# Feed-forward of a three-layer block: the first product takes both token halves together

## What is computed

```python
def sqrelu_mlp(h, w1, w2):
    return jnp.square(jax.nn.relu(h @ w1)) @ w2

    x = x + sqrelu_mlp(rms_norm(x, norm_ffn), w1, w2)   # w1: 1024 x 4096, w2: 4096 x 1024
return rms_norm(x, final_norm)
```

## Time and profile before

| | |
|---|---|
| time, median of 3 (lowest to highest) | 2796.82 us (2793.5 to 2798.48) |
| span of the profiled execution | 2797.9 us |
| TensorE busy | 2662.8 us, 95% |
| its weight loads | 2224.8 us, 80% |
| VectorE busy | 1160.3 us, 41% |
| ScalarE busy | 853.9 us, 31% |
| feed-forward's matmuls | from 2088.69 us to about 2790.3 us |

### The profile page before, as it was taken

One profiled execution on the slowest core, in us unless ns is written; L12 is line 12 of the kernel. 1 busy time (PEld: TensorE's weight loads), 2 busy tenths in 40 slices (PEclk: granted clock), 3 DMA queues, 4 the chain that ended last, 5 costly groups with the idle time before them and its releaser, 6 DMA issues. The chain is left out here.

```text
span 2797.9 us, 36557 instructions
## 1 busy us (share of the span) xinstructions
PE 2662.8 (95%) x13360; PEld 2224.8 (80%) x13360; DVE 1160.3 (41%) x2217; ACT 853.9 (31%) x1567; POOL 419.4 (15%) x890
## 2 busy tenths in 40 slices
PE   7999999998997999999979899999889999999998
PEld 6888888887786987777767588887668888888887
DVE  4433333323322410566644566665333333333333
ACT  4322222212212422444433443442332211122112
POOL 3444444432000204000001011011000000000000
PEclk9999999999998999999989899999899999999999
DMA  4211111102422221011034101100433111111111
GB/s 152 69 59 47 58 47 58 47 24 82 149 106 81 90 83 51 33 40 36 19 119 145 65 31 50 57 24 33 150 117 128 38 45 51 46 60 40 42 52 67
DMA packets 71391, 188.38 MB, mean 67 GB/s; under 512 B 7744, under 2 KB 29184, under 8 KB 70400
## 3 DMA queue, kind: packets, MB, share of 16 engines
q1 hardware_dynamic: 71296, 187.11, 20.3%
HBM read 149.34 MB, written 37.75 MB: 67 GB/s over the span
## 5 line engine op out<-in xcount | busy, mean ns | idle before, releaser
L527 PE MATMUL ra_qkv_ps<-ra_wh,ra_xl 128*128 (+1 forms) x512 | 206.7, 404 | 3.9 <-DVE ra_wl L420 3.9
L2513 PE MATMUL ff_f_ps<-x_upper,ff_w1l 128*128 128x512 f32 x512 | 200.5, 392 | 6.5 <-DVE ff_w1l L2449 6.5
L527 PE MATMUL ra_qkv_ps<-ra_wh,ra_xh 128*128 (+1 forms) x512 | 200.3, 391 | 0.0
L2513 PE MATMUL ff_f_ps<-x_lower,ff_w1h 128*128 128x512 f32 x512 | 200.2, 391 | 0.0
L2513 PE MATMUL ff_f_ps<-x_upper,ff_w1h 128*128 128x512 f32 x512 | 200.1, 391 | 0.0
L527 PE MATMUL ra_qkv_ps<-ra_wl,ra_xh 128*128 (+1 forms) x512 | 199.9, 390 | 0.0
L2526 PE MATMUL ff_y_ps<-ff_w2h,ff_hl 128*128 128x512 f32 x512 | 199.2, 389 | 0.0
L2526 PE MATMUL ff_y_ps<-ff_w2l,ff_hh 128*128 128x512 f32 x512 | 199.2, 389 | 0.0
L2526 PE MATMUL ff_y_ps<-ff_w2h,ff_hh 128*128 128x512 f32 x512 | 199.2, 389 | 0.0
L2476 DVE TENSOR_TENSOR ff_acc<-ff_y_ps,ff_acc 128x1024 f32<-128x1024 f32 x64 | 78.4, 1225 | 213.9 <-PE ff_y_ps L2526 213.9
L527 PE MATMUL ra_gate_ps<-ra_wh,ra_xl 128*128 (+1 forms) x512 | 156.0, 305 | 0.0
(11 more groups left out here) (391 smaller groups left out, 6582.2 us busy)
## 6 DMA issues: line engine op xcount, KB each, us to landing
staging<-in_w_ff SPq DMA_DIRECT2D x64, 512.0 KB, 3.9
ra_raw<-in_w_in_a SPq DMA_DIRECT2D x32, 768.0 KB, 4.6
gated_a<-ra_sg SPq DMA_DIRECT2D x64, 128.0 KB, 1.9
staging<-in_w_out_a SPq DMA_DIRECT2D x16, 512.0 KB, 3.8
staging<-in_w_vr_c SPq DMA_DIRECT2D x16, 512.0 KB, 4.0
wa_gin<-gated_a SPq DMA_DIRECT2D x6, 1024.0 KB, 5.0
staging<-in_x SPq DMA_DIRECT2D x8, 512.0 KB, 3.9
wa_xin<-in_x SPq DMA_DIRECT2D x8, 512.0 KB, 4.6
```

Source lines behind the costliest of these rows:

```text
L527: last = pe.matmul(out, a[:, kt, t * P:(t + 1) * P], b[:, ds(slot, 1), kt, at:at + n].rearrange("p a n -> p (a n)"), start=(kt == 0 and i ...
L2513: last = pe.matmul(f_ps[j % 2][:, :], a[:, kt, f * P:(f + 1) * P], b[:, kt, half * HALF:(half + 1) * HALF], start=(kt == 0 and i == 0), st ...
```

## The change

The first product takes a group of features f for both token halves at once: 48 matmuls into two banks in turn, so that each w1 piece is the stationary operand of two matmuls (w1l) or four (w1h) that follow each other, and their outputs alternate between two banks. There are four banks for it instead of two. Group numbers j now run over f = j // 2 and half = j % 2; TensorE signals once for a pair (`f_mm` counts to 4 a chunk). The second product's wait for the activations stands, for row tile 0 alone, inside its loop over f. The work behind a group and the places of the weight pieces in the order are as they were.

```diff
-        f_ps = [... for i in range(2)]
+        f_ps = [... for i in range(4)]
@@ scalar
-                act.activation(hh[:, j % 4, j // 4 * HALF:(j // 4 + 1) * HALF], f_ps[j % 2][:, :], ACT.Copy).then_inc(hh_done, 1)
+                act.activation(hh[:, j // 2, j % 2 * HALF:(j % 2 + 1) * HALF], f_ps[j % 4][:, :], ACT.Copy).then_inc(hh_done, 1)
...
-                    act.wait_ge(f_mm, 8 * c + j + 1)
-                    act.activation(relu[:, :], f_ps[j % 2][:, :], ACT.Relu).then_inc(relu_done, 1)
+                    act.wait_ge(f_mm, 4 * c + j // 2 + 1)
+                    act.activation(relu[:, :], f_ps[j % 4][:, :], ACT.Relu).then_inc(relu_done, 1)
...
@@ vector: square_of and h_lower with f_ps[j % 4], hl[:, j // 2, half j % 2]
@@ tensor
-            def inner(c, j):
+            def inner(c, f):
                 first = type(c) is int and c == 0
-                if j >= 2 or not first:
-                    pe.wait_ge(hl_done, 8 * c + j - 1)
-                f, half = j % 4, j // 4
+                if f >= 2 or not first:
+                    pe.wait_ge(hl_done, 8 * c + 2 * f - 2)
                 for kt in range(KT):
-                    if first and j == 0 and kt % 2 == 0:
+                    if first and f == 0 and kt % 2 == 0:
                         pe.wait_ge(wl_done, kt // 2 + 1)
                     for i, (a, b) in enumerate(((w1l, xh), (w1h, xl), (w1h, xh))):
-                        last = pe.matmul(f_ps[j % 2][:, :], a[:, kt, f * P:(f + 1) * P], b[:, kt, half * HALF:(half + 1) * HALF],
-                                         start=(kt == 0 and i == 0), stop=(kt == KT - 1 and i == 2))
+                        for half in range(2):
+                            last = pe.matmul(f_ps[2 * (f % 2) + half][:, :], a[:, kt, f * P:(f + 1) * P],
+                                             b[:, kt, half * HALF:(half + 1) * HALF],
+                                             start=(kt == 0 and i == 0), stop=(kt == KT - 1 and i == 2))
                 last.then_inc(f_mm, 1)
             def outer(c, t):
-                if t % 4 == 0:
-                    pe.wait_ge(hl_done, 8 * c + t + 4)
                 if t >= 2 or type(c) is not int:
                     pe.wait_ge(y_added, NT * c + t - 1)
                 for f in range(FT):
+                    if t == 0:
+                        pe.wait_ge(hl_done, 8 * c + 2 * f + 2)
```

More of the change, by code:

```diff
@@ L2349, in feed_forward @@
         rms = sb("rms", [P, NT])
-        f_ps = [ctx.enter_context(nc.psum_tensor(f"ff_f_ps{i}", [P, HALF], F32)) for i in range(2)]
+        f_ps = [ctx.enter_context(nc.psum_tensor(f"ff_f_ps{i}", [P, HALF], F32)) for i in range(4)]
         y_ps = [ctx.enter_context(nc.psum_tensor(f"ff_y_ps{i}", [P, 2, HALF], F32)) for i in range(2)]
@@ L2425, in _ @@
             with act.Fori(1, NC) as c:
-                act.wait_ge(f_mm, 8 * c)
+                act.wait_ge(f_mm, 4 * c)
                 for n in range(4):
@@ L2457, in square_of @@
                 dve.wait_ge(relu_done, 8 * c + j + 1)
-                dve.scalar_tensor_tensor(f_ps[j % 2][:, :], f_ps[j % 2][:, :], 0.0, relu[:, :], ALU.max,
+                dve.scalar_tensor_tensor(f_ps[j % 4][:, :], f_ps[j % 4][:, :], 0.0, relu[:, :], ALU.max,
                                          ALU.mult).then_inc(sq_done, 1)
@@ L2462, in h_lower @@
                 dve.wait_ge(hh_done, 8 * c + j + 1)
-                at = (j % 4, slice(j // 4 * HALF, (j // 4 + 1) * HALF))
-                dve.tensor_tensor(hl[:, at[0], at[1]], f_ps[j % 2][:, :], hh[:, at[0], at[1]].bitcast(F32),
+                at = (j // 2, slice(j % 2 * HALF, (j % 2 + 1) * HALF))
+                dve.tensor_tensor(hl[:, at[0], at[1]], f_ps[j % 4][:, :], hh[:, at[0], at[1]].bitcast(F32),
                                   ALU.subtract).then_inc(hl_done, 1)
@@ L2528, in outer @@
                 last.then_inc(y_mm, 1)
-            for j in range(8):
-                inner(0, j)
+            for f in range(FT):
+                inner(0, f)
             pe.wait_ge(wl_done, 8)
@@ L2536, in _ @@
                 pe.wait_ge(wl_done, 8 * c + 4)
-                for j in range(8):
-                    inner(c, j)
+                for f in range(FT):
+                    inner(c, f)
                 pe.wait_ge(wl_done, 8 * c + 8)
```

## The result

The changed kernel takes 2850.07 us (median of 4 runs, 2845.14 to 2851.41), against 2797.65 us for the kernel before on the same footing: a ratio of 1.0186, with an interval of 1.0168 to 1.0203. The forecast was 2849 us.

What follows compares the result with a forecast made beforehand. TensorE, busy 95% of the span and alone in the feed-forward, was taken to bound the kernel. 2797.9 + 36.2 + 0 + 18.3 - 2.5 = 2849.9 us, span 1.1 us above the median, so 2849 us; own range 2841 to 2855, with rivals 2826 to 2857.

Steps and rivals of the forecast that it cites:

- sign (e): Expected in the changed trace: 226.7 ns between matmul starts inside the first product at full clock.
- (a): Before each second product: TensorE waits for the last weight piece, 4.52 us a chunk, +36.2 us over eight chunks.
- (b): Second product, row tile 0: the wait for activations before f = 3 is covered by 2 us, cost 0.
- (c): Behind each of eight TensorE stops: clock falls to half, 2.3 us a stop, +18.3 us.
- the three stretches: Half-clock stretches of 5.5, 3.3 and 5.8 us behind idle times of 3.20, 4.23 and 4.62 us, used to price the clock.
- slices of the last quarter below 9: Expected in the changed trace's feed-forward stage: TensorE's clock below 9 tenths in the slices of the last quarter.
- (d): Start of the feed-forward stage: six matmuls for each kt, so TensorE doesn't starve for w1 pieces, -2.5 us.
- (e): First product's four banks, emptied in time, and later w1 loads, covered by the second product: cost 0.

Runs made afterwards that it cites:

- e3: e2 with each kt's three matmuls of one token half before the other's three, so the bank changes every third matmul; 2796.72 us, ratio 1.0002 to before.
- e2: e1 with row tile 0 waiting before each f for the lower token half alone, row tile 4 for all eight groups; 2796.14 us, ratio 0.999 to before.
- e8: Changed kernel with 10 further unused matmuls a chunk ahead of TensorE's wait for weight piece 7; 2834.48 us, ratio 1.0126.
- e6: Kernel before, with only weight piece 7 moved from behind group 6 to behind group 7; 2854.86 us, ratio 1.0192.
- e5: Changed kernel with TensorE's wait for all eight weight pieces split, one piece ahead of each f of row tile 0; 2821.18 us, ratio 1.0078.
- e4: Changed kernel with 19 more unused matmuls a chunk ahead of TensorE's wait for weight piece 7; 2831.18 us, ratio 1.0121.
- e1: Changed kernel with weight piece 7 made behind group 5 instead of group 6 on ScalarE and VectorE; 2802.29 us, ratio 1.0016 to before.
- e7: Changed kernel with weight piece 7 made behind group 7 instead of group 6; 2866.42 us, ratio 1.0244.

## Why the prediction was right

- **Matmuls at an unchanged 226.7 ns** (sign (e)): right. 43.53 us for 192 in the changed kernel, and e3 against e2 for the order alone. This rested on rows in which a repeated operand came with the same bank; a repeated operand with another bank behaves the same.
- **(a), the stop**: said 4.26 us idle and 36.2 us in all; measured 4.25 us in chunk 0, 4.44 in the other seven, 37.4 us in all. The step that was short by 0.19 us is the last hand-over, from w2l to TensorE: 0.04 us was taken from a wait that a matmul itself holds. In the loop of the changed kernel 0.23 us pass, in its chunk 0 0.04. In chunk 1 a register operation of TensorE's weight-load queue (L2521) stands at 2232.4 us, between the end of w2l (2232.32) and the first weight load (2232.53). In chunk 1 of e8 none stands there, and the hand-over is 0.04 us in the loop too, for the same wait; so it is in e6, with the old order. That the register operation is the cause was not tried by itself.
- **(b), the wait for the activations covered**: right, by e5, and its price if uncovered 2.4 us a chunk instead of 2.2.
- **(c), the clock**: said 18.3 us, measured 17.4, and 19 us between the changed kernel and e4 in the medians. All eight stops had it. That the size came out so near is in part luck, since one of the three stretches was misread. The 5.8 us one does not begin behind the stop of 4.62 us: the clock was at half before that stop began, from 2080.9 us on, within a stop of 3.60 us ahead of it:

```profile
2082.10:2084.00 1.90, 1.90 (x8) 1.56 (x8) 0.00 (x0) 0.60 (x1) 0.00 (x0) 0.50 0.00 0
2084.10:2088.60 4.50, 0.00 (x0) 0.00 (x0) 2.67 (x5) 3.15 (x5) 0.00 (x0) 0.50 0.00 0
```

The other two stretches alone (5.5 and 3.3 us) would have given 16.5 us. The sign "slices of the last quarter below 9" did not come: they are all 9, as a slice is 71 us long.
- **(d), the start**: said -2.5 us, measured -2.4 (and -2.5 and -2.3 in e2 and e3). TensorE's waits for `ff_w1l` go from three (6.5 us) to the first one alone (4.6 us). In e6, with the old order, the first product of chunk 0 takes 49.6 us.
- **(e), banks and loads at nothing**: right; the first products of chunks 1 to 7 take 43.53 us, and ScalarE never waits for the load of a w2 piece in the changed kernel. The text counts one pair of groups between pieces 5 and 7; it is two (96 matmuls, the 21.8 us it gives), so the reading stands.

Each term was within 1.2 us, and the errors of +1.2, -0.9 and +0.1 us largely cancel: that the total came within about 1 us is luck too, the mechanism is not.

The version without stops, e2, has the lowest median of all kernels here, 0.999 (0.9981 to 1.0) of before, and is not told apart from e3. The 2.5 us in the stage is what the idea can bring, since behind the start of chunk 0 TensorE waited for nothing in the kernel before.

## What to carry to other kernels

When two units of work that ended one behind the other are made to end together, look at what was placed between them on the other engines: its cover was the second unit, and it is now on the path. Move it ahead of the merge, and let each wait ask for no more than its reader reads. Price a stop of TensorE with the clock behind it, from rows of the same trace; here that was another half of the stops' own length (17.4 us beside 35.3).

## What the runs showed of the hardware

- The granted clock and the length of a stop, in the profiled execution of each kernel: 0.66 us idle (e1) never made it fall, 2.0 us (e8) behind two stops of eight, 2.15 us (e5) behind four of eight, 4.25 to 4.44 us (changed kernel) behind eight of eight. A stop of the same length filled with matmuls (e4) left the clock alone.
- A stop of 6.4 us (e7) cost no more by the clock than one of 4.4 us (second products of 45.6 to 45.7 us against 45.4 to 46.6); in chunk 1 of e7 2.7 us at half clock lie in the idle time.
- A matmul of 512 columns with its own weight load starts every 226.7 ns at the full clock, whether the stationary operand is repeated or not and whether the bank changes or not (e2, e3). At half clock it is 427 ns, so the full clock's 226.7 ns are some 13 ns more than half of that.
